# The final combining pass moved beside the last two expert blocks, their rows formed from PSUM

## What is computed

```
hmid = silu(xb @ w_gate[e]) * (xb @ w_up[e])      # per block, xb: gathered normalised rows
out  = hmid @ w_down[e]
h    = h + gate0 * out_row0 + gate1 * out_row1    # per token
y    = h * rsqrt(mean(h * h) + eps) * w_final     # per token
```

## Time and profile before

| | us |
|---|---|
| median of 3 runs | 1505.07 (1504.49 to 1506.98) |
| the profiled execution | 1505.11 |
| its span | 1503.4 |
| PE busy | 1416.1 (94%) |
| DVE busy | 1061.5 (71%) |
| ACT busy | 766.1 (51%) |
| POOL busy | 568.4 (38%) |

### The profile page before, as it was taken

The page is one execution under the profiler, slowest core; times in us unless marked ns, Lnnn a source line. Parts: engine busy times, 40 slices in busy tenths (PEclk is TensorE's granted clock), DMA queues, the critical chain, the costliest instruction groups (busy, mean ns, idle before and its releaser), DMA issues. The chain is left out here.

```text
span 1503.4 us, 21686 instructions
## 1 busy us (share of the span) xinstructions
PE 1416.1 (94%) x7625; PEld 1233.0 (82%) x7625; DVE 1061.5 (71%) x1225; ACT 766.1 (51%) x891; POOL 568.4 (38%) x345
## 2 busy tenths in 40 slices
PE   6999999999999999899999659999999999999976
PEld 5999999999999998788877548888888888888852
DVE  6687722366666664545463579999999999999956
ACT  6332222333333335344433438777777777777734
POOL 2323324454444442485644014333433333333311
PEclk9999999999999999999999669999999999999997
DMA  5222333234444445876653659999999999999958
GB/s 197 65 78 86 126 95 111 80 130 143 144 141 147 138 144 167 294 219 239 209 168 130 231 201 383 402 396 390 377 381 362 389 379 383 385 388 387 369 211 343
DMA packets 115793, 361.07 MB, mean 240 GB/s; under 512 B 18772, under 2 KB 48468, under 8 KB 99348
## 3 DMA queue, kind: packets, MB, share of 16 engines
q1 hardware_dynamic: 100164, 322.37, 58.6%
q0 software_dynamic: 15568, 37.87, 7.3%
HBM read 316.52 MB, written 59.64 MB: 250 GB/s over the span
## 5 line engine op out<-in xcount | busy, mean ns | idle before, releaser
L2048 DVE TENSOR_TENSOR wgu_l<-wgu,wgu_h 128x2048 fp32r<-128x2048 f32 x128 | 290.0, 2288 | 27.4 <-ACT wgu_h L1928 26.5
L1928 ACT CAST wgu_h<-wgu 128x2048 fp32r<-128x2048 f32 x124 | 237.4, 1915 | 100.6 <-PE bank0and L64 100.5
L62 PE MATMUL bank0and<-wgu_h,xh_blk 128*128 128x512 f32 x512 | 203.7, 398 | 2.9 <-DVE xl_blk L2052 2.9
L64 PE MATMUL bank0and<-wgu_h,xl_blk 128*128 128x512 f32 x512 | 200.9, 392 | 0.0
L62 PE MATMUL bank0and<-xh,wh 128*128 128x352 f32 x576 | 197.6, 343 | 3.0 <-ACT raw L906 3.0
L63 PE MATMUL bank0and<-wgu_l,xh_blk 128*128 128x512 f32 x512 | 200.3, 391 | 0.0
L64 PE MATMUL bank0and<-xh,wl 128*128 128x352 f32 x576 | 186.7, 324 | 0.0
L63 PE MATMUL bank0and<-xl,wh 128*128 128x352 f32 x576 | 186.5, 324 | 0.0
L1671 POOL TENSOR_TENSOR wol<-wo,woh 128x1024 fp32r<-128x1024 f32 x48 | 121.4, 2536 | 123.5 <-ACT woh L996 123.5
L1835 POOL DMA_INDIRECT scratch_picked<-yb,dst x31 | 92.7, 2991 | 197.5 <-DVE yb L2042 197.5
L2057 DVE TENSOR_TENSOR wd_l<-wd,wd_h 128x1024 fp32r<-128x1024 f32 x128 | 148.2, 1219 | 1.2 <-ACT wd_h L1934 1.0
(11 more groups left out here) (496 smaller groups left out, 3234.5 us busy)
## 6 DMA issues: line engine op xcount, KB each, us to landing
wgu<-in_w_gate_up SPq DMA_DIRECT2D x128, 1024.0 KB, 7.6
wd<-in_w_down SPq DMA_DIRECT2D x128, 512.0 KB, 7.6
wo<-in_w_out SPq DMA_DIRECT2D x48, 512.0 KB, 4.9
w<-in_w_in_tiles SPq DMA_DIRECT2D x36, 512.0 KB, 3.6
yy<-scratch_picked SPq DMA_DIRECT2D x8, 1024.0 KB, 12.6
scratch_xb<-stage POOLq DMA_DIRECT2D x10, 512.0 KB, 4.0
xb<-scratch_xb SPq DMA_DIRECT2D x8, 640.0 KB, 4.4
scratch_uT<-feat SPq DMA_DIRECT2D x8, 528.0 KB, 5.0
```

What stands on the lines that cost most here:

```text
L62: nc.tensor.matmul(acc, lh, rh, start=start, stop=False)
L64: return nc.tensor.matmul(acc, ll, rh, start=False, stop=stop)
L1928: nc.scalar.copy(wgu_h[:, s], wgu[:, s]).then_inc(gu_high, 1)
L2048: nc.vector.tensor_tensor(wgu_l[:, s], wgu[:, s], wgu_h[:, s].bitcast(F32), ALU.subtract).then_inc(gu_split, 1)
```

## The change

`combine` is gone as a block; its work is written into the programs of `experts`.

- The last two blocks are neither copied to SBUF nor scattered. Two extra tiles, 9 and 10, hold their rows: Pool gathers for each the tokens' h rows (from `h`), gates (from a new DRAM table `gates`) and the other choice's row (from `picked`); DVE adds gate times that row, then gate times the PSUM result (`add_late`). A token can have a row in both blocks: tile 9's sums are therefore scattered to `h`, and tile 10 gathers its h rows after that has landed.
- `picked` rows of the two last blocks are set to zero by two scatters of a zeroed `yb` early in the loop. Stores of all tiles are indirect: a token with a row in the last two blocks gets a row number out of bounds in its plain tile (`out_row`), and is stored by tile 9 or 10 alone. Tile 10's store waits for all stores before it.
- SP stores the gates, and loads `w_final` and four h tiles, before the loop; two h tiles before the last down weights, three behind; the `yy` loads wait for the scatter of the last block but two, and for the places that they take.
- PE sums tiles 2, 4, 6, 7; DVE sums 8, 1, 0, 3, 5.

```diff
+            sp.wait_ge(rows_ready, 2)
+            for k in range(2):
+                sp.dma_start(S["gates"][k * T:k * T + SEQ, :].rearrange("(t p) k -> p t k", p=P), gate3[:, 0:NT, k:k + 2]).then_inc(gates_stored, 16)
+                sp.dma_start(S["gates"][k * T + SEQ:k * T + T, :].rearrange("(t p) k -> p t k", p=TS), gate3[0:TS, NT:NT + 1, k:k + 2]).then_inc(gates_stored, 16)
+            sp.dma_start(w_final[:], A["norm_final_w"][0].partition_broadcast(P)).then_inc(h_loaded, 16)
+            for t in range(FIRST):
+                sp.dma_start(h[t], S["h"][t * P:t * P + P, :]).then_inc(h_loaded, 16)
             with sp.Fori(0, m) as i:
                 load_gate_up(i + 2)
                 load_down(i + 1)
+            sp.wait_ge(gu_split, m * 4 + 8)
+            load_h(NT)
+            load_h(4)
             load_down(m + 1)
+            for t in (5, 6, 7):
+                load_h(t)
             sp.wait_ge(y_stored, m * 16 + 32)
+            for t in (8, 1, 0, 2, 3, 4, 5, 6, 7):
+                used = 0 if t == 0 else (t + 1) // 2
+                if used:
+                    sp.wait_ge(gu_used, m * 4 + (4 + used))
+                sp.dma_start(yy[t][0:live(t)], picked[t * P:t * P + live(t)]).then_inc(loaded[t], 16)
...
-            gather(1)
-            gather(2)
+            gather(1, 1)
+            for j in range(2):
+                if j:
+                    pool.wait_ge(y_stored, 16)
+                then_own(pool, nc.gpsimd.tensor_copy(dst[:], of_row[:, 1, bass.ds(m + (1 + j), 1)]), index_copied, j + 2)
+                pool.indirect_dma_start(out=S["picked"], out_offset=bass.IndirectOffsetOnAxis(ap=dst[:], axis=0),
+                                        in_=yb[:], in_offset=None, bounds_check=2 * T - 1, oob_is_err=False).then_inc(y_stored, 16)
+            gather(2, 4)
...
-            scatter(m)
-            scatter(m + 1)
+            scatter(m, m * 2 + 5)
+            then_own(pool, nc.gpsimd.memset(late_gate[:], 0.0), zeroed, 3)
+            for j in range(2):
+                for k in range(3):
+                    nc.gpsimd.tensor_copy(late_row[:, j, k:k + 1], of_row[:, k, bass.ds(m + (1 + j), 1)]).then_inc(zeroed, 1)
...
+            for j in range(2):
+                late_gather(j, late_gate[:, j, :], S["gates"], 1)
+            late_gather(0, h[NT + 1], S["h"])
+            pool.wait_ge(xT_psum, m * 2 + 6)
+            pool.wait_ge(y_stored, m * 16 + 48)
+            late_gather(0, other[0], S["picked"], 2)
+            pool.wait_ge(down_split, m * 4 + 12)
+            pool.wait_ge(xg_loaded, m * 16 + 112)
+            late_gather(1, other[1], S["picked"], 2)
+            pool.wait_ge(h_loaded, 16 * (NT + 2))
+            pool.wait_ge(y_done, m + 2)
+            pool.indirect_dma_start(out=S["h"], out_offset=bass.IndirectOffsetOnAxis(ap=late_row[:, 0, 0:1], axis=0),
+                                    in_=total[0], in_offset=None, bounds_check=T - 1, oob_is_err=False).then_inc(y_stored, 16)
+            store(0)
+            pool.wait_ge(y_stored, m * 16 + 64)
+            late_gather(1, h[NT + 2], S["h"])
+            for n in range(1, NT + 3):
+                if ORDER[n] == NT + 2:
+                    pool.wait_ge(out_stored, 16 * n)
+                store(n)
...
-            unload_y(m)
             low_down(m + 1, range(2, 4))
-            dve.wait_ge(down_used, (m + 1) * 4 + 4)
-            nc.vector.tensor_copy(xg[:], S["banks45"][:]).then_inc(y_done, 1)
+            add(NT)
+            dve.wait_ge(y_stored, m * 16 + 32)
+            add_late(0, 96)
+            add(1)
+            norm(NT)
+            norm(9)
+            add(0)
+            norm(1)
+            add_late(1, 128)
+            norm(0)
+            norm(2)
+            add(3)
+            norm(10)
+            norm(4)
+            norm(3)
+            add(5)
+            norm(5)
+            norm(6)
+            norm(7)
...
+            def add_late(j, loads):
+                dve.wait_ge(xg_loaded, m * 16 + loads)
+                dve.wait_ge(down_used, (m + j) * 4 + 4)
+                after(nc.vector.scalar_tensor_tensor(out=h[NT + 1 + j], in0=other[j], scalar=late_gate[:, j, 1:2], in1=h[NT + 1 + j],
+                                                     op0=ALU.mult, op1=ALU.add))
+                nc.vector.scalar_tensor_tensor(out=total[j], in0=(S["banks23"], S["banks45"])[j][:], scalar=late_gate[:, j, 0:1],
+                                               in1=h[NT + 1 + j], op0=ALU.mult, op1=ALU.add).then_inc(y_done, 1)
...
+                if n == 0:
+                    pe.wait_ge(diag_ready, 2 * len(ON_PE))
+                    pe.wait_ge(hT_done, m + 2)
+                if 2 <= n < 4:
+                    pe.wait_ge(y_done, m + (n - 1))
...
-ON_PE = [1, 3, 5, 7]
-ORDER = [8, 0, 1, 2, 3, 4, 5, 6, 7]
+ON_PE = [2, 4, 6, 7]
+ON_DVE = [8, 1, 0, 3, 5]
+ORDER = [8, 9, 1, 0, 2, 10, 4, 3, 5, 6, 7]
```

More of the change, by code:

```diff
@@ L1763, in experts, with live, psum_of, is_loaded @@
         y_done, y_stored = sem("y_done"), sem("y_stored")
-        holder = C["holder"]
+        loaded = [sem(f"final_loaded{t}") for t in range(NT)]
+        loaded, loaded_at = loaded + [loaded[1]], [16, 32, 16, 16, 16, 16, 16, 16, 32]
+        h_loaded, out_stored = sem("h_loaded"), sem("out_stored")
+        summed, rms, out_ready = (sem(n) for n in ("summed", "rms", "out_ready"))
+        diag_ready, pe_summed = sem("diag_ready"), sem("pe_summed")
+        holder = C["holder"]
+        def live(t):
+            return TS if t == NT else P
+        def psum_of(t, half):
+            return bank[(0, 6, 2, 4, 0)[ON_PE.index(t)] + half][:, :]
+        def is_loaded(eng, t):
+            eng.wait_ge(h_loaded, 16 * (NT + 2))
+            eng.wait_ge(loaded[t], loaded_at[t])
         block = ctx.enter_context(nc.Block())
@@ L2039, in unload_y @@
             def unload_y(i):
-                wait(dve, y_stored, i * 16)
+                dve.wait_ge(y_stored, i * 16 + 32)
                 dve.wait_ge(down_used, i * 4 + 4)
@@ L2182, in add, with make_diag @@
+            def make_diag(n):
+                for k in range(2):
+                    nc.vector.tensor_scalar(diag[n // 2][:, n % 2, k, :], C["ident"][:], S["gate"][:, ON_PE[n], k:k + 1], None, ALU.mult).then_inc(diag_ready, 1)
             def add(t):
-                r = rows_of(t)
-                dve.wait_ge(loaded[t], loaded_at[t])
+                r = live(t)
+                is_loaded(dve, t)
                 for k in range(2):
@@ L2204, in norm @@
                                                          op0=ALU.mult, op1=ALU.mult)
                 ins.then_inc(out_ready, 1)
-            for n, t in enumerate(ON_PE):
-                for k in range(2):
-                    nc.vector.tensor_scalar(diag[:, n, k, :], C["ident"][:], S["gate"][:, t, k:k + 1], None, ALU.mult).then_inc(diag_ready, 1)
-            add(NT)
-            add(0)
-            norm(NT)
-            for t in range(2, NT, 2):
-                add(t)
-                norm(t - 2)
-                norm(t - 1)
@@ L2226 @@
     "z": (T, D), "xb": (T, D + GROUPS * NSTATE), "bct": (2 * GROUPS * NSTATE, T), "uT": (D, T), "v": (T, D), "yT": (D, T),
-    "h": (T, D), "hn": (T, D), "picked": (2 * T, D),
+    "h": (T, D), "hn": (T, D), "picked": (2 * T, D), "gates": (2 * T, 2),
 }
```

238 lines of the change are left out of this document (122 added, 116 removed).

## The result

The changed kernel took 1524.76 us (median of four runs, 1520.14 to 1525.04) beside 1506.03 of the kernel before on the same chip: 1.0117 times as long, 95% interval 1.0095 to 1.014. Forecast were 1502.7 and at most 1509.5. The profiled execution took 1520.14 us with a span of 1518.1, 17.1 over the forecast span of 1501.0. A second profile of the same kernel, nearer to the median, has a span of 1524.2.

The account below looks back on a forecast made before the run. Bound taken: the chain of waits ending in the combining pass, with a barrier stretch before it. S 1473.5 plus 22.0, then 0.9 + 3.3 + 1.0, gave 1500.7; plus 0.3, span 1501.0; time 1502.7, range 1497.5 to 1509.5.

Parts of the forecast that it names:

- the 0.3 I took: Start of the expert stage: four more small DVE steps make TensorE start about 0.3 us later, added to the span.
- S: Tail: moment tile 10's gathered h rows have landed, releasing DVE's second late addition; forecast 1473.5, break-even 1475.9.
- So nothing is the taken value, 3 us the upper bound: Start of the expert stage: gate stores, w_final and h loads ahead of block 2's weights cost nothing, at most 3 us.
- lead of 6.3 us: Start of the expert stage: ACT takes block 2's first weights 6.3 us after their landing, without idling.
- at most 7 us: Start of the expert stage: block 2's first weights come at most 7 us later behind SP's added transfers.
- I take 6.0, nearer to the loaded end: Tail: landing of tile 9's scatter to h takes 6.0 us, between 3.3 with empty queues and 7.7 loaded.
- taken 6.1: Tail: tile 10's gather of h rows lands 6.1 us after issue, between 4.4 with empty queues and 8.4.
- Rival 3: Tail: scatter to h and gather both at the loaded end, 7.7 and 8.4; S 1477.5, time 1506.7; chance within forecast's 0.47.
- 1.0 from there to the end: Program end: 1.0 us from the final indirect store's landing to the end of the span.
- as long after it as at the barrier would add 1.9: Program end: a drain after the final store as long as at the barrier adds 1.9 us, left in the range.
- Rival 2: Tail: DVE additions hold Pool's indirect issue, as in the loop (7.20 us); S 6.2 later, time 1508.9; chance 0.15.
- rival 5: Tail: Pool stays busy after each indirect issue (6.3 us); eleven stores need 69 us, some 40 more; chance 0.05.

Follow-up runs that it names:

- a0: The changed kernel run again without edits, as yardstick for the other runs: 1525.23 us, ratio to the kernel before 1.0129.
- x1: Changed kernel with the four gate stores moved behind SyncE's last h loads and two gate gathers behind GpSimd's first `picked` gather: 1523.46 us, ratio to before 1.012.
- x2: Changed kernel with w_final and the first four h tiles loaded at the end of the loop, gate stores left at the start: 1524.70 us, ratio to before 1.0136.
- x13: Changed kernel with gates stored as 256 pieces (other tokens' gates) instead of 8-byte pieces, h loads left at the start: 1516.04 us, ratio to before 1.0057.
- x5: Changed kernel without tile 9's scatter to h, tile 10's h rows gathered early (some tokens lose a row): 1518.35 us, ratio to before 1.009.
- x7: Kernel before with the combining pass written into the experts' block, so only the barrier is gone: 1507.74 us, ratio to before 1.0017.
- x12: Kernel before without the barrier, combining pass in the experts' block, and y stored by SyncE instead of GpSimd: 1498.48 us, ratio to before 0.9949.

## Why the prediction was wrong

By its own steps, in the first profile: span 1518.1 against 1501.0, +17.1. The start of the stage adds 6.6 beyond the 0.3 I took (scatter 29 at 570.6 instead of 563.7, +6.9), the chain to S 5.3, the end 6.0; the front was 0.7 us faster and VectorE from S on 0.1. a0's profile, whose span is 6.1 us longer, has 3.6 of that in the start of the stage and 2.0 ahead of it.

- **"So nothing is the taken value, 3 us the upper bound"** for the start failed. The lead of 6.3 us was read rightly (6.8 in the table of leads), and so was the delay of the issue: the additions were bounded at 15.0 us together and held SyncE's queue for 15.0 (885.6 to 900.6), so block 2's weights were issued some 7 us later ("at most 7 us"). What failed is the landing behind them, left at the 4.9 us of queues that were not full (0.87 in the table by stretches). It took 10.9. Seven us and six are 13, some 7 more than the lead, and scatter 29 came 6.9 later. Landings of block 2's first weights rose as much where there was no stall (x1 9.6, x2 9.0, x13 11.0); there the issue came at most 2 us later, counted from the first weight split, so they were just in time. Even with the 4.9, 7 us against 6.3 was no ground for "nothing". The time could not be won back behind it: before too, TensorE was busy all through the loop.
- **"I take 6.0, nearer to the loaded end" and "taken 6.1"** failed by size. Both transfers took 7.6, the loaded end of the range; the addition before them was 1.5 us late, since from the first `yy` issue to tile 8's addition it took 9.0 us and not 5.96. In the rows no gathers stood beside the `yy` loads, here four were issued between 1448.6 and 1454.1; that they are the cause was not tried. Rival 3 (S 4.0 later) is what happened, and a little more. The mechanism, a wait of VectorE on the row of h, was right (x5).
- **"1.0 from there to the end"** failed, and the escape, a drain "as long after it as at the barrier would add 1.9", failed with it. I read the barrier's 6.49 us as running from the last issue beside its landing. It starts when GpSimd gets to it, here behind the wait for the last store, and is then 6.8 long. Both rows were in hand: 5.3 us for 64 DMAs and 0.78 for 9 are the same 0.08 each.
- **Right**: no barrier and `yy` issued 7.8 us behind the scatter (7.6 forecast); S to VectorE's end 21.9 us (22.0); ScalarE's last squares one behind the other. Rival 2 did not come: GpSimd's issues beside the additions took 0.96 to 1.27 us, but for one gather with 3.22, behind which the scatter to h still left 0.88 us after its addition. Nor did rival 5: stores follow each other within 1.3 to 1.5 us.
- What the change was to bring, the barrier's 3.1 us, was no idle time to be had: the barrier paid the drain where x7 and the changed kernel pay it at the end. Only x12, where another queue stores the output, gets it.

## What to carry to other kernels

Where transfers are added ahead of prefetched weights, sum them all against the one lead there is, and take the weights' landing as it is behind full queues (here 9 to 11 us instead of 4.9). A store of many 8-byte pieces spends the lead though it moves almost nothing. Behind it look at two things: how long the lead takes to come back (here some 12 blocks), and whether the engine that sets the pace has any idle time, without which the stall itself is never made up. Let GpSimd finish early: it owes its drain for every DMA it issued, so the last stores belong on a queue that owes none. Before removing a barrier, ask what its slowest instruction does, and where the same work will be done without it.

## What the hardware showed that I had not expected

GpSimd's drain took 0.053 us and 0.082 per DMA issued since the drain before, whatever the kind, the bytes and the time since. SyncE's took 0.007 to 0.13 us in all these kernels. The Trainium skill, page "VectorE: DVE Perf Modes", section "The DRAIN you can't avoid", calls the drains at a program's start and end a constant of some 12 ns on all engines; SyncE's 7 ns is near that, GpSimd's 6768 ns is not, and the measurement decides.

The store of 17 KB in 2112 pieces of 8 bytes held SyncE's queue for 7.8 us at the start, and for 14 us in x1, beside full queues.
